# A two-part, four-layer transformer step: output products of the heads written feature-major, softmax scaling moved ahead of the transposes, lower weight halves written over the landed weights, splits three chunks ahead

## The chip, the cores and the metric

The kernel runs on one core of one Trainium2 chip. A core has TensorE (PE: matmul, with its weight loads shown apart as PEld), VectorE (DVE), ScalarE (ACT), GpSimd (POOL), SyncE (SP, here only the issuer of loads) and 16 DMA engines. Each engine works through its own list of instructions in order; they meet through semaphores. The metric is the device time of one execution in microseconds.

## The reference

Batch 1, 256 tokens, width 1024, float32. Part one has two layers, part two two more.

```
part one, per layer (first a layer norm of the input x):
  h = x @ w_in: differential heads (4 of 128), windowed heads with a bias (8 of 64),
      a gated 3-tap convolution, and 3 gates
  mix = sum over branches of sigmoid(gate_b) * (branch_b @ w_branch_b);  mix @ w_mix_out
  x = layer_norm(alpha*x + mix)
  cross-attention to mem (4 heads of 256: xa_q, xa_kv, xa_o);  x = layer_norm(alpha*x + .)
  ffn: silu(conv3(x@w_g)) * (x@w_u) @ w_out (inner width 2816);  x = layer_norm(alpha*x + .)
part two, per layer:
  x += 0.5 * swiglu(rms_norm(x));   x += 0.5 * swiglu(rms_norm(x))   (around the mixer)
  h = rms_norm(x) @ w_in_2: pooling, moba (4 heads of 64, causal here: one block of 256),
      dilated (4 heads of 64: 3 dilations merged in one softmax), 31-tap convolution module
  x += concat(pool, moba, dil, conv) @ w_out_2
out = rms_norm(x)
```

With 256 tokens the mask of a moba and of a dilated head is causal: queries 0 to 127 see keys 0 to 127 alone.

## The kernel before

**Weights as chunks.** All weights are cut into 336 chunks of 128 x 2048 float32 (1 MB), in order of use, and `mem` is one more chunk in each layer of part one. `plan()` (L97) lists the chunks and puts the heads' steps at chunk positions. A chunk is landed in `raw` by SyncE (L631), in one of three slots (`RING`, L32). ScalarE copies it to `whi` in the rounded matmul type fp32r (L728), VectorE subtracts to get the lower half `wlo` = `raw` - `whi` (L1317). TensorE then multiplies (L1022, `product`): for each block high x high, high x low and low x high, 48 matmuls of 128x128 by 256 columns for one chunk; all matmuls are recorded at the helper's line L989. Kind F gives features in rows, kind T tokens in rows, B and O are the branch and output products. An O chunk adds to the four banks of `accM`, one per pair of feature tiles.

**Who splits when.** While TensorE works on chunk `pos`, ScalarE and VectorE go through the same list: they take the result of chunk `pos-1` (`take`), do those steps of `pos` whose names are in `BEFORE_SPLIT`, split chunk `pos+2` (`split_at(pos + 2)`), and do the other steps. The second chunk after the last one of each group that ends in a norm (key `ends`) is split on GpSimd in place of VectorE (`by_pool`, L429 and L702), eleven in all. SyncE's load of chunk n waits until chunk n-3 is split.

**Norms.** At a chunk with `ends`, VectorE adds each of the four banks to x (L1357 in part one, L1360 in part two), ScalarE squares (L747), VectorE adds the squares (L1350). In part two the norm's scaling is put off to the results, and `xh`, `xl` (upper and lower half of x) are made at once (L741, L1335), so that the next chunk can start. In part one TensorE first sums x and the squares, spreads the factors, and x is scaled and shifted (L1395, L1401) before the next product.

**Heads.** A head has four steps, at positions one apart. *scores*: TensorE multiplies queries and keys, VectorE takes the maximum (for windowed, moba and dilated heads after adding a bias, L1639, L1642), ScalarE takes the exponential and sums each row in `ew` and `rsum` (L909). *turn*: TensorE transposes `ew`, four blocks of 128x128, into `turnP` (L1176); ScalarE copies it to `eT` (L915). *mix*: TensorE multiplies with `eT` as the weights and the values as the moving side, so that tokens stand in the rows; VectorE divides by the row sum (L1675, L1678) into `otok`. *back*: TensorE transposes `otok` into `outP` (L1203), for two heads of 64 features together; ScalarE and VectorE make the upper and lower half (L935; L1685, L1694) that the next product reads. A differential head scales `ew` by its row sums already after scores (L1651 to L1659), and has a norm of its own at mix.

TensorE's own steps of a position are spread over its product as hooks; those that the product needs (`needs`) come ahead of it. A bank is claimed by `Bank.claim`, which waits for its last reader. During O chunks the heads use the bank `outP`, since `accM` is taken.

**The second part's mixer** is the chunks `cg`, `ca`, `qm`, `km`, `qd`, `kd`, `up`, `vm`, `vd`, and then four of `wo`. VectorE also computes the 31-tap convolution there, in six groups of steps (`taps`, L1704; two operations per tap), one group at each of the positions `qm` to `vd`; on VectorE `taps` comes behind the split of its position. The convolution's own norm (`cstats`, `cspread`) uses `outP` at the first two `wo` chunks.

## Time and profile before

| | |
|---|---|
| three runs | 2282.15, 2287.42, 2293.49 us; median 2287.42 |
| profiled execution | 2269.32 us, its span 2267.5 us |
| TensorE | 2138.3 us busy, mean granted clock 0.974 |
| VectorE | 1436.8 us busy (63%) |
| ScalarE | 1009.3 us busy (45%) |
| GpSimd | 99.7 us busy (4%) |
| DMA | 366 MB, 161 GB/s over the span |

The rows used below name a line of the kernel, an engine, the operation, what it writes and what it reads, and how often. Matmuls overlap, so the duration of a single one is longer than its distance to the next. In a timeline "idle before" with an arrow says how long the engine had nothing to do and what ended that. The chain of waits is followed back from the last instruction; each of its pieces is a stretch in which one kind of work let the end wait.

### The profile page before, as it was taken

How to read it: one execution, taken by the hardware profiler on the slowest of the kernel's cores; microseconds unless marked ns; L12 is line 12 of the kernel's file. 1: busy time of each engine (PE TensorE's matmuls, PEld its weight loads, DVE VectorE, ACT ScalarE, POOL GpSimd, SP SyncE). 2: the span in 40 equal slices, each digit the busy share in tenths (PEclk: the TensorE clock that was granted, in tenths of full speed). 3: DMA queues.
4: the chain of work that ended last, by engine and by line, in shares of the span. 5: the costliest groups of instructions: out<-in, count | busy, mean ns of one | idle time of the engine just before them, and what ended most of it. 6: DMA issues, size and time to landing. Idle time of an engine off the chain costs nothing.

```text
span 2267.5 us, 39445 instructions
## 1 busy us (share of the span) xinstructions
PE 2138.3 (94%) x17460; PEld 2080.3 (92%) x17460; DVE 1436.8 (63%) x1690; ACT 1009.3 (45%) x1166; POOL 99.7 (4%) x69
## 2 busy tenths in 40 slices
PE   7999999899899999989997999879999999979998
PEld 6899999899899999989997999769999999868997
DVE  5665554666765656457776756866666666765665
ACT  4544454444445443544444434334444444234443
POOL 1000010100100000010001000001000000000000
PEclk9999999999999999999998999989999999989999
DMA  5444543355444455435552554323554555213542
GB/s 198 148 162 163 204 162 143 133 185 189 149 149 165 146 188 191 152 112 216 186 189 104 199 192 175 112 75 135 204 203 149 209 200 186 112 68 115 209 186 94
DMA packets 52858, 366.08 MB, mean 161 GB/s; under 512 B 5904, under 2 KB 5904, under 8 KB 9296
## 3 DMA queue, kind: packets, MB, share of 16 engines
q1 hardware_dynamic: 52272, 361.21, 43.3%
q8 instruction: 138, 2.26, 0.4%
q0 software_dynamic: 416, 2.35, 0.3%
q14 instruction: 32, 0.26, 0.0%
HBM read 362.49 MB, written 1.05 MB: 160 GB/s over the span
## 4 chain that ended last, share of the span: by engine, by line
PE 76%; DVE 10%; issue 9%; ACT 3%; POOL 1%; DMA 0%; POOLq 0%; ACTq 0%; DVEq 0%
PE accM L989 43%; PE scoreP L989 17%; PE outP L989 8%; PE turnP L989 7%; DVE wlo L1317 2%; DVE yc L1704 1%; ACT whi L728 1%; PE turnP L1176 1%; DVE xl L1335 1%; ACT ew L909 1%; DVE acc L1350 1%; PE outP L1203 0%; DVE cen L1395 0%; DVE cen L1401 0%; DVE mrs L1646 0%
## 5 line engine op out<-in xcount | busy, mean ns | idle before, releaser
L1317 DVE TENSOR_TENSOR wlo<-raw,whi 128x2048 fp32r<-128x2048 f32 x325 | 744.1, 2290 | 411.5 <-ACT whi L728 411.0
L728 ACT ACTIVATE whi<-raw 128x2048 fp32r<-128x2048 f32 x336 | 640.4, 1910 | 256.4 <-PE accM L989 169.9
L989 PE MATMUL accM<-xh,whi 128*128 128x256 f32 x1152 | 338.9, 294 | 16.8 <-DVE xl L1415 10.9
L989 PE MATMUL scoreP<-xh,whi 128*128 128x256 f32 x1152 | 325.9, 283 | 17.8 <-DVE xl L1415 9.0
L989 PE MATMUL accM<-xl,whi 128*128 128x256 f32 x1152 | 324.9, 282 | 0.0
L989 PE MATMUL accM<-xh,wlo 128*128 128x256 f32 x1152 | 324.9, 282 | 0.0
L989 PE MATMUL scoreP<-xl,whi 128*128 128x256 f32 x1152 | 323.7, 281 | 0.0
L989 PE MATMUL scoreP<-xh,wlo 128*128 128x256 f32 x1152 | 323.5, 281 | 0.0
L989 PE MATMUL accM<-fh,whi 128*128 128x256 f32 x1056 | 293.2, 278 | 0.7 <-DVE wlo L1317 0.7
L989 PE MATMUL accM<-fh,wlo 128*128 128x256 f32 x1056 | 293.1, 278 | 0.0
L989 PE MATMUL accM<-fl,whi 128*128 128x256 f32 x1056 | 293.1, 278 | 0.0
L989 PEld LDWEIGHTS accM<-xh,whi 128*128 128x128 f32 x1152 | 220.7, 192 | 27.6 <-issue 27.3
L989 PEld LDWEIGHTS scoreP<-xh,whi 128*128 128x128 f32 x1152 | 220.7, 192 | 19.4 <-issue 18.7
L989 PEld LDWEIGHTS accM<-xl,whi 128*128 128x128 f32 x1152 | 220.5, 191 | 2.7 <-issue 2.5
L989 PEld LDWEIGHTS accM<-xh,wlo 128*128 128x128 f32 x1152 | 221.9, 193 | 0.0
L989 PEld LDWEIGHTS scoreP<-xh,wlo 128*128 128x128 f32 x1152 | 221.7, 192 | 0.0
L989 PEld LDWEIGHTS scoreP<-xl,whi 128*128 128x128 f32 x1152 | 220.6, 192 | 0.2
L989 PEld LDWEIGHTS accM<-fh,wlo 128*128 128x128 f32 x1056 | 199.6, 189 | 0.0
L989 PEld LDWEIGHTS accM<-fh,whi 128*128 128x128 f32 x1056 | 198.2, 188 | 0.9 <-DVE wlo L1317 0.9
L989 PEld LDWEIGHTS accM<-fl,whi 128*128 128x128 f32 x1056 | 198.2, 188 | 0.0
L989 PE MATMUL turnP<-xh,whi 128*128 128x256 f32 x480 | 133.1, 277 | 0.0
L989 PE MATMUL turnP<-xl,whi 128*128 128x256 f32 x480 | 133.1, 277 | 0.0
(264 smaller groups left out, 4297.2 us busy)
## 6 DMA issues: line engine op xcount, KB each, us to landing
raw<-in_W SPq DMA_DIRECT2D x336, 1024.0 KB, 4.8
biasr<-in_bias SPq DMA_DIRECT2D x16, 256.0 KB, 2.7
raw<-in_memT SPq DMA_DIRECT2D x2, 1024.0 KB, 4.7
cc<-in_consts POOLq DMA_DIRECT2D x1, 1536.0 KB, 6.7
x<-in_xT SPq DMA_DIRECT2D x4, 256.0 KB, 4.4
out<-x SPq DMA_DIRECT2D x4, 256.0 KB, 2.5
c<-in_consts SPq DMA_DIRECT2D x1, 464.5 KB, 6.1
par<-in_par POOLq DMA_DIRECT2D x2, 203.5 KB, 3.7
```

What stands on the lines that cost most here:

```text
L728: nc.scalar.activation(whi[:, slot(c), :], raw[:, n % RING, :], ACT.Copy).then_inc(split_hi.sem, 1)
L909: ins = nc.scalar.activation(ew[:, e0 + i, :], src, ACT.Exp, bias=negmax[:, e0 + i:e0 + i + 1], scale=scale, accum_out=rsum[:, s0 + i:s0 + ...
L989: return nc.tensor.matmul(dst, a, b, start=start, stop=stop, skip_group_check=True)
L1176: ins = nc.tensor.transpose(turnP[:, k * S + t * P:k * S + (t + 1) * P], src[t][:, k * P:(k + 1) * P], ident)
L1317: v.tensor_tensor(wlo[:, slot(c), :], raw[:, n % RING, :], whi[:, slot(c), :].bitcast(F32), ALU.subtract).then_inc(split_lo.sem, 1)
L1335: ins = v.scalar_tensor_tensor(xl[:, k, :], x[:, k, :], gain(n, k), xh[:, k, :].bitcast(F32), ALU.mult, ALU.subtract)
L1350: v.tensor_tensor(accq, a, sq[:, b % 2, :], ALU.add).then_inc(summed.sem, 1)
L1704: ins = v.scalar_tensor_tensor(yc[:, m, :], src, w, yc[:, m, :], ALU.mult, ALU.add)
```

## The change

1. `raw` gets five slots and `whi` four. `wlo` also has five, and lies at the same addresses as `raw`: VectorE's subtract writes the lower half over the landed chunk. So the load of chunk n waits until the product n-5 is finished, not for a split.
2. Splits are made three chunks ahead (`LEAD`), two ahead at a chunk that ends in a norm. The second chunk after such a chunk then brings two splits. GpSimd splits no more; `by_pool` and `pool_lo` are gone.
3. Windowed, moba, dilated and cross-attention heads: VectorE multiplies `ew` by the inverse row sums at *turn* (new semaphore `evened`), and TensorE's transposes wait for it. At *mix* the values are the weights and `eT` the moving side, so that features stand in the rows. Two heads of 64 features share one bank, which turns with the banks of `accM` (`outP` in O chunks) and is kept until *back*. The scaling to `otok` and the transposes of *back* go; ScalarE and VectorE read the halves straight from the bank. Differential heads are unchanged.
4. Moba and dilated heads leave out the block of queries 0 to 127 against keys 128 to 255: scores, bias, exponential, transposes (three, not four) and the second matmul of the output product are that much smaller; the maximum is taken by two instructions in place of one.
5. In part two *back* moves from the third position after scores to the second, and what `wo` 1 and `wo` 2 need ahead of their product is now *mix*.

```diff
-RING = 3
+RAW_RING = 5
+HI_RING = 4
+LEAD = 3
...
+        raw = sb("raw", [P, RAW_RING, CH], where=landing)
+        landing.close()
+        wlo = sb("wlo", [P, RAW_RING, CH], F32R)
+        whi = sb("whi", [P, HI_RING, CH], F32R)
...
+                if name == "mix" and what["kind"] not in ("diff", "xa") and what["j"] % 2:
+                    mix_bank[what["n"]] = mix_bank[what["n"] - 1]
+                elif name == "mix" and c["kind"] in ("F", "T"):
...
+        def lead(pos):
+
+            return pos + LEAD - 1 if pos < len(chunks) and "ends" in chunks[pos] else pos + LEAD
...
-                if c["c"] >= RING:
-                    await_split(sp, c["c"] - RING)
+                r = raw_slot(c)
+                if c["c"] >= RAW_RING:
+                    old = chunks[c["c"] - RAW_RING]
+                    if old["kind"] == "M":
+                        await_split(sp, old["c"])
+                    else:
+                        await_chunk(sp, old)
...
-                if c["c"] + 2 in by_pool:
-                    n = c["c"] + 2
-                    pool.wait_ge(split_hi.sem, split_hi.at(n))
-                    nc.gpsimd.tensor_tensor(wlo[:, slot(chunks[n]), :], raw[:, n % RING, :],
...
-                    split_at(pos + 2)
+                    split_at(lead(pos))
...
-                        pe.wait_ge(expd.sem, expd.at(n))
+                        pe.wait_ge(evened.sem, evened.at(n))
...
+                            if kind in ("moba", "dil"):
+                                if k > t:
+                                    continue
+                                at = (k + t) * P
...
+                    elif kind == "xa":
+                        for d in range(2):
+                            for k in range(2):
+                                ins = mm(mix_bank[n][1][:, d * S:(d + 1) * S], v[:, k, v0 + d * P:v0 + (d + 1) * P],
+                                         e[:, k * S:(k + 1) * S], k == 0, k == 1)
+                    else:
+                        rows = slice(64 * (j % 2), 64 * (j % 2) + 64)
+                        late = P if kind != "win" else 0
+                        o = mix_bank[n][1]
+                        mm(o[rows, 0:S], v[:, 0, v0:v0 + w], e[:, 0:S], True, False)
+                        ins = mm(o[rows, late:S], v[:, 1, v0:v0 + w], e[:, S:2 * S - late], False, True)
...
+                mine = [s for s in steps.get(pos, []) if s[0] in PE_STEPS
+                        and (s[0] != "back" or s[1]["kind"] == "diff")]
...
+                elif name == "turn" and what["kind"] != "diff":
                     n, kind, j = what["n"], what["kind"], what["j"]
...
+                    dve.wait_ge(expd.sem, expd.at(n))
+                    s = mrs[:, 10 + 2 * (j % 2):12 + 2 * (j % 2)]
+                    i0 = sum_column(kind, j)
+                    v.reciprocal(s, rsum[:, i0:i0 + 2]).then_inc(inverted.sem, 1)
+                    dve.wait_ge(inverted.sem, inverted.at(n))
                     for t in range(2):
...
+                        e = ew[:, 2 * (j % 2) + t, keys(kind, t)]
+                        last = v.tensor_scalar(e, e, s[:, t:t + 1], None, ALU.mult)
+                    last.then_inc(evened.sem, 1)
```

## Rows read from the trace of the kernel before

**Rows 1.** The page, part 1: busy time and share of each engine.
```profile
...
PE 2138.3 (94%) x17460; PEld 2080.3 (92%) x17460; DVE 1436.8 (63%) x1690; ACT 1009.3 (45%) x1166; POOL 99.7 (4%) x69
...
```

**Rows 2.** The chain of waits, whole span: start us, us, work.
```profile
...
432.31 5.65 PE turnP L989 x48
...
1029.47 5.44 PE turnP L989 x48
...
```

**Rows 3.** Waits of TensorE, whole span: waited for, us in total, times, longest.
```profile
...
PE accM L989 <- DVE wlo L1317: 0.7, 1, 0.7
...
```

**Rows 4.** The page, part 6: KB of each load, us to landing.
```profile
...
raw<-in_W SPq DMA_DIRECT2D x336, 1024.0 KB, 4.8
...
```

**Rows 5.** Groups by line: out<-in, count, busy us, mean ns.
```profile
...
L1317 DVE TENSOR_TENSOR wlo<-raw,whi 128x2048 fp32r<-128x2048 f32 x325 | 744.1, 2290 | 411.5 <-ACT whi L728 411.0
...
L702 POOL TENSOR_TENSOR wlo<-raw,whi 128x2048 fp32r<-128x2048 f32 x11 | 50.6, 4602 | 1354.8 <-ACT whi L728 1354.8
...
```

**Rows 6.** Timeline at the norm ahead of a mixing stage: start, us.
```profile
...
1406.03 4.59 POOL L702 TENSOR_TENSOR wlo<-raw,whi 128x2048 fp32r<-128x2048 f32 x1 [176.49 <-ACT whi L728]
...
1407.41 3.89 DVE L1335 SCALAR_TENSOR_TENSOR xl<-x,par,xh 128x256 fp32r<-128x256 f32 x2
...
1411.82 0.87 DVE L1335 SCALAR_TENSOR_TENSOR xl<-x,par,xh 128x256 fp32r<-128x256 f32 x2
...
```

**Rows 7.** Timeline at a norm of part one.
```profile
...
1001.08 2.44 DVE L1350 TENSOR_TENSOR acc<-sq 128x512 f32<-128x512 f32 x1
...
1004.18 0.73 PEld L989 LDWEIGHTS turnP<-x,ones 128*128 128x128 f32 x4 [0.26 <-DVE x L1357]
...
```

**Rows 8.** Timeline around the transposes of cross-attention and window heads.
```profile
...
336.62 2.29 DVE L1317 TENSOR_TENSOR wlo<-raw,whi 128x2048 fp32r<-128x2048 f32 x1 [2.89 <-ACT whi L728]
...
354.83 0.69 DVE L1685 TENSOR_TENSOR ol<-outP,oh 128x512 fp32r<-128x512 f32 x1 [0.68 <-ACT oh L935]
...
354.20 0.59 ACT L935 ACTIVATE oh<-outP 128x512 fp32r<-128x512 f32 x1
...
122.28 0.48 DVE L1691 SCALAR_TENSOR_TENSOR yl<-outP,small,yh 128x256 fp32r<-128x256 f32 x1 [1.52 <-ACT yh L935]
...
122.29 0.60 PE L1176 MATMUL turnP<-c,ew 128*128 128x128 f32 x4
...
```

**Rows 9.** The chain of waits around heads.
```profile
...
338.46 0.44 PE turnP L1176 x4
...
344.56 1.73 PE scoreP L989 x8
...
124.94 1.06 PE scoreP L989 x4
...
134.17 4.62 PE accM L989 x38
...
```

**Rows 10.** Groups by line: VectorE's scaling operations.
```profile
...
L1655 DVE TENSOR_SCALAR ew<-ew,mrs 128x256 f32<-128x256 f32 x16 | 4.9, 350 | 0.3
...
L1675 DVE RECIPROCAL mrs<-rsum 128x2 f32<-128x2 f32 x40 | 6.6, 164 | 52.5 <-PE outP L989 31.8 <-PE accM L989 20.6
...
```

**Rows 11.** Timeline of the first mixing stage.
```profile
...
1474.00 4.54 DVE L1704 SCALAR_TENSOR_TENSOR yc<-hpad,par,yc 128x256 f32<-128x256 f32 x10
...
1474.81 0.99 PE L1176 MATMUL turnP<-c,ew 128*128 128x128 f32 x4 [3.98 <-ACT eT L915]
...
1520.61 0.69 PE L1203 MATMUL outP<-c,otok 128*128 128x128 f32 x2 [3.82 <-DVE yc L1719]
1525.00 1.30 PE L989 MATMUL outP<-v,eT 128*128 128x64 f32 x5 [3.69 <-DVE zl L1694]
...
1544.58 0.36 PE L989 MATMUL accM<-zh,whi 128*128 128x256 f32 x1 [1.02 <-DVE zl L1694]
...
```

**Rows 12.** Windows of the second mixing stage: busy us by engine, clock, DMA.
```profile
...
1979.00:1989.00 10.00, 5.22 (x36) 4.36 (x34) 6.93 (x10) 6.99 (x13) 0.00 (x0) 0.90 0.04 16
1989.00:1999.00 10.00, 10.00 (x35) 7.88 (x35) 6.34 (x13) 1.85 (x6) 0.00 (x0) 0.50 0.23 91
...
```

More of the change, by code:

```diff
@@ L70 @@
 NC0 = _at
-NC2 = 4 * 512 + 512 + 512
+TRI = P + S
+NC2 = 4 * 512 + 2 * TRI
 class Signal:
@@ L242, in plan @@
             at(base + 10, "cspread", l)
-            order = dict(rot=1, cstats=2, cspread=2, pool=2, back=3, mix=4, turn=5, scores=6, poolw=7, taps=8,
+            order = dict(rot=1, cstats=2, cspread=2, pool=2, mix=3, back=4, turn=5, scores=6, poolw=7, taps=8,
                          csquare=9)
@@ L262, in sem @@
             return ctx.enter_context(nc.semaphore(name))
-        raw = sb("raw", [P, RING, CH])
-        whi = sb("whi", [P, RING, CH], F32R)
-        wlo = sb("wlo", [P, RING, CH], F32R)
+        landing = ExitStack()
+        raw = sb("raw", [P, RAW_RING, CH], where=landing)
+        landing.close()
+        wlo = sb("wlo", [P, RAW_RING, CH], F32R)
+        whi = sb("whi", [P, HI_RING, CH], F32R)
         x = sb("x", [P, KT, S])
@@ L425, in kernel_program @@
         cs = [c["c"] for c in chunks]
-        landed = [sem(f"landed{i}") for i in range(RING)]
+        landed = [sem(f"landed{i}") for i in range(RAW_RING)]
         split_hi = sig("split_hi", cs)
-        by_pool = [c["c"] + 2 for c in chunks if "ends" in c and c["c"] + 2 < len(chunks)]
-        split_lo = sig("split_lo", [c for c in cs if c not in by_pool])
-        pool_lo = sig("pool_lo", by_pool)
+        split_lo = sig("split_lo", cs)
         def await_split(engine, c):
-            signal = pool_lo if c in by_pool else split_lo
-            engine.wait_ge(signal.sem, signal.at(c))
+            engine.wait_ge(split_lo.sem, split_lo.at(c))
         used = sig("used", [c["c"] for c in products if "ends" not in c])
@@ L506, in kernel_program @@
             for name, what, *_ in steps.get(c["c"], []):
-                if (name == "scores" and what["kind"] == "diff") or (name == "mix" and what["kind"] != "diff"):
+                if (name == "scores" and what["kind"] == "diff") or (name == "turn" and what["kind"] != "diff"):
                     inverse_order.append(what["n"])
@@ L513, in kernel_program @@
         weighed = sig("weighed", [n for n in stage["scores"] if hs[n]["kind"] == "diff"])
+        evened = sig("evened", [n for n in stage["turn"] if hs[n]["kind"] != "diff"])
         inverted = sig("inverted", inverse_order)
@@ L517, in kernel_program @@
         mixed = sig("mixed", stage["mix"])
-        oscaled = sig("oscaled", stage["mix"])
+        oscaled = sig("oscaled", [n for n in stage["mix"] if hs[n]["kind"] == "diff"])
         o2 = sig("o2", [n for n in stage["mix"] if hs[n]["kind"] == "diff"])
@@ L521, in kernel_program @@
         oroot = sig("oroot", [n for n in stage["mix"] if hs[n]["kind"] == "diff"])
-        backed = sig("backed", stage["back"])
+        backed = sig("backed", [n for n in stage["back"] if hs[n]["kind"] == "diff"])
         back_hi = sig("back_hi", stage["back"])
@@ L592, in head_place, with keys, laid @@
             return (zh, zl)[part][:, (2 if kind == "moba" else 4) + j // 2, :]
+        def keys(kind, t):
+            return slice(0, P) if t == 0 and kind in ("moba", "dil") else slice(0, S)
+        def laid(kind, t):
+            if kind in ("moba", "dil"):
+                return slice(0, P) if t == 0 else slice(P, TRI)
+            return slice(t * S, (t + 1) * S)
         def sum_column(kind, j):
@@ L860, in take @@
                 elif r == "su":
-                    split_at(pos + 2)
+                    split_at(lead(pos))
                     hidden(c)
@@ L1200, in step @@
                     pe.wait_ge(oscaled.sem, oscaled.at(n))
-                    for d in range(2 if kind == "xa" else 1):
-                        for t in range(2):
-                            ins = nc.tensor.transpose(outP[:, d * S + t * P:d * S + (t + 1) * P],
-                                                      otok[:, t, d * P:(d + 1) * P], ident)
+                    for t in range(2):
+                        ins = nc.tensor.transpose(outP[:, t * P:(t + 1) * P], otok[:, t, 0:P], ident)
                     ins.then_inc(backed.sem, 1)
@@ L1247, in needs @@
                 if c["role"] == "wo":
-                    return (name, what["kind"] if name == "back" else "") in {
-                        0: [("poolw", "")], 1: [("back", "moba")], 2: [("back", "dil")], 3: [("cspread", "")]}[c["j"]]
-                return c["role"] == "xo" and name == "back" and what["j"] == c["j"]
+                    return (name, what["kind"] if name == "mix" else "") in {
+                        0: [("poolw", "")], 1: [("mix", "moba")], 2: [("mix", "dil")], 3: [("cspread", "")]}[c["j"]]
+                return c["role"] == "xo" and name == "mix" and what["j"] == c["j"]
             hooks = {}
@@ L1316, in split @@
                     return
-                v.tensor_tensor(wlo[:, slot(c), :], raw[:, n % RING, :], whi[:, slot(c), :].bitcast(F32),
+                v.tensor_tensor(wlo[:, raw_slot(c), :], raw[:, raw_slot(c), :], whi[:, hi_slot(c), :].bitcast(F32),
                                 ALU.subtract).then_inc(split_lo.sem, 1)
@@ L1693, in step @@
                     else:
-                        v.tensor_tensor(lo, outP[:, 0:S], hi.bitcast(F32), ALU.subtract).then_inc(back_lo.sem, 1)
+                        v.tensor_tensor(lo, mix_bank[n][1][:, 0:S], hi.bitcast(F32), ALU.subtract)\
+                            .then_inc(back_lo.sem, 1)
                 elif name == "trig":
```

154 lines of the change are left out of this document (81 added, 73 removed).

## The prediction

> **What bounds the kernel now.** I read the page's busy shares first: TensorE works in 94% of the span [rows 1]. The chain of waits says how: in long stretches it is one product after another, 48 matmuls in 5.44 us in some of them and 5.65 us in others [rows 2]. At 5.44 us the 336 products need 1828 us of the 2267.5; 440 us are norms, heads, waits and the slower pace. The densest part of it is the mixing of the second part.
>
> Next the waits. TensorE waited for the lower half of a weight chunk once, 0.7 us in all [rows 3]. So deeper buffers and a third chunk of lead take away no wait that TensorE has. They can pay only through what moves with them.
>
> **Splits, rings and lead.** Five landing slots with the lower part written over them give the load of chunk n the start "product n-5 finished". Before it was "chunk n-3 split", which fell in about the same moment, but the split is now wanted a chunk earlier. A load lands 4.8 us after its issue [rows 4], a product lasts 5.44: ScalarE may wait up to 1 us for it, and TensorE wants the data three products later. I take 0, bounds 0 to +3 us, as the load just fits and the reserve of three products would have to be gone first.
>
> **The split leaves GpSimd.** Eleven lower halves were computed there, 4.60 us each [rows 5], at the moment when VectorE takes the norm's residual. They collide. In the second part GpSimd ran from 1406.03 to 1410.62 and VectorE's pair of `xl` operations took 3.89 us where its neighbours take 0.87 [rows 6]. The next product starts with this `xl`, so it is on the path. By the same row 3.0 us go at the norms that follow products 212, 258 and 291, and 2.0 at 225 and 304, where the collision is later: 13 us. In the first part an `acc` operation took 2.44 us in place of its normal 0.69 (what `x` and other operations of this size take), but TensorE was summing x meanwhile and waited 0.26 us for it [rows 7]. The squares come 1.8 us earlier, of which TensorE's own sums leave some 0.6: four norms make 2.4 us, and I give the two after `mo` nothing, since products lie beside them. Bounds for all six: 0 to 1.75 each.
>
> The Trainium skill (SBUF — State Buffer, "Who interferes with whom") states that a VectorE instruction with two SBUF inputs and a GpSimd instruction that reads SBUF exclude each other for the whole instruction. The trace agrees: the `xl` pair ends 0.7 us after GpSimd's subtract, while the residual with one input from PSUM beside it keeps 0.69 us. By the rule, the gain would be whole as soon as GpSimd has no such work, as I sum it.
>
> VectorE takes these eleven splits, 2.29 us each [rows 5]. They are done one chunk before the norm, and the place of the extra one is the catch-up: two splits in a row at the second chunk after the norm. In the feed-forward VectorE has room (63% busy over the span), so 0. In the mixing it has none; that is counted below.
>
> **Heads without the turn back.** Transposes cost TensorE 0.11 us each (four in 0.44) [rows 9]. Dropped: 4 per cross-attention head, 2 per pair of others. A cross-attention output product stays 8 matmuls of 256 columns. A window head's was 8 matmuls of 64 columns, 1.09 us (4.62 less 30 of a product at 0.1177); now it is 4 of 256 columns: between half of the 1.73 that eight take in cross-attention and the 1.06 of four score matmuls [rows 9]. So 0 to 0.2 us gained per head; I take 0.1.
>
> In exchange the transposes of every such head now wait for VectorE: reciprocal and two scalings (0.20, and twice 0.35 overlapping to 0.62, for 256 columns: 0.8 us; 0.76 where one is of 128) [rows 10]. What matters is what VectorE has queued before them.
>
> Cross-attention, first layer [rows 8]. Head 0: the transposes came at 338.46 [rows 9]; VectorE subtracts a weight chunk from 336.62 to 338.9 and is then ready with the head at 339.7: +1.3. Head 1: no transposes-back stand ahead any more, so its transposes move from the middle to the start of their product, about 353.5. But VectorE's program has the lower half of head 0 first, which waits for ScalarE's `oh`, and this for the copy of a product that ends only then: 354.83 + 0.69 + 0.8 = 356.3, a stall of 2.8, less 0.44 saved. Head 2 meets the same order with half a product in between: 1.5 late, less 0.44. The turns back of heads 2 and 3 save 0.9. Sum +3.8 a layer, **+7.6 us** for two; bounds 0 to +12.
>
> Window heads [rows 8]: head 0's transposes at 122.29 now wait behind `yl` (122.28 + 0.48), until 123.7: +1.3. Heads 3 and 5 meet `yl` in the same way, +0.4 each; the others have 1 to 2 us to spare. Less 0.9 for transposes and 0.8 for eight products: +0.4 a layer, **+0.8 us**; bounds -4 to +8.
>
> **The mixing stages** [rows 11]. From the norm ahead of the first (1407.41) to the start of its last product (1544.58) 137 us pass, in which 12 products need 65; the second is alike. At their start VectorE is the bound: each product brings a split (2.29), ten tap operations (4.54) and 1.4 to 2 us of rotation, over 8 us against a product's 5.44. The catch-up split comes there: +2.2 against the 3.0 that the norm gives back. Then the new wait bites. The transposes of moba 0 and 1 stood at about 1468.8 and at 1474.81; now they wait until VectorE has done a split (it may start when ScalarE is ready, about 1471), taps, a rotation and the scaling: 1479.0 and 1479.8. TensorE turns the second at 1480.8, +6.0. The scores behind come 4 to 5 us later, the transposes of moba 2 and 3 wait for the last taps (until 1495.2), and the product `vd` ends 4.7 late. From here it is regained. Triangular scores save 0.2 a head, the transposes 0.1, products some 0.4. Above all the turn back goes: before, TensorE waited 3.82 us for `outP` to be free for two transposes that it no longer has, then 3.69 us for `zl` behind the whole convolution norm, and 1.02 us at the last product. Now the convolution's spread goes about 3.2 late, at 1519.0. The first output product of the dilated heads follows the bank's release at about 1522.6 in place of 1525.0. `wo 1` ends at 1531.4 (before 1535.6), `wo 2` starts at 1538.3 (before 1544.6). So -6.3 in each stage, the norm's 3.0 included.
>
> The clock takes part of it back. In the second stage TensorE worked 5.22 of the 10 us from 1979, and in the 10 us after them it had a granted clock of 0.50, which is 1.2 GHz [rows 12]. Around the turns of moba 0 and 1 the first stage's idle time grows from 5 to 11 us, and I add 3 us there; the second paid that already. I take **-3.3 and -6.0**, bounds -12 to +5 each.
>
> **Sum**, against the profiled execution's own 2269.3 us: norms -2.4 and, outside the mixing, -3.0 -2.0 -2.0; cross-attention +7.6; windows +0.8; mixing -9.3. That is -10.3, or 2259. The other executions of before lie higher: the median is 2287.4, 18.1 above the profiled one. I lay the difference on the median: 2287.4 - 10.3, **2277 us**. The kernel's measurements can't tell less than about 0.5% (11.4 us) from no change, and this forecast lies just inside that.
>
> **Rivals.**
> (1) The waits hurt less, and GpSimd's collision more: VectorE gets through the mixing early enough, and only the gains are left (norms -15, mixing with -10 each, heads 0). The norm's 6 in the mixing is in both, so -29, of which 4 stay for windows and cross-attention: -25, 2262 us. For it: the pair of 3.89 us is ahead of TensorE's next product. Against it: the taps really stand ahead of the scaling in VectorE's program.
> (2) The scaling before the transposes costs more than the turn back gave. Its place is every non-differential head; its price per head is what VectorE has ahead, a split (2.29) or a group of taps (4.54). With 6 us more in each mixing stage, 6 in each cross-attention and 4 in each window stage, less the norms' 15, it is about +12 + 12 + 8 - 15 = +17 us: 2304. It decides once the late transposes of moba 2 and 3 carry on into the convolution's norm, that is if `cspread` comes more than 9 us late. For it: VectorE's queue is full there. Against it: the waits of 3.8 and 3.7 us stand right behind.
> (3) TensorE's pace. It ran the same feed-forward program at 5.65 us a product in the first layer and at 5.44 in the second (at 432.31 and 1029.47) [rows 2], and nothing in the chain says why. Six such stretches of 32 products are worth 6.7 us each. If two or three fall the other way, it is 2277 plus or minus 16.
> (4) The deeper lead does nothing and neither does the rest: 2287. That is near to my sum and can't be told from it by the time.
>
> **Chances.** Forecast, within 7 us of 2277: 0.40. Rival 1: 0.20. Rival 2: 0.15. Rival 3: 0.14, half each way. Rival 4: 0.11. Under 2276 (faster) lie rival 1, half of 3 and two fifths of the forecast's spread: 0.43. Over 2298.9 (slower): rival 2 and a little of 3: 0.17. The rest, 0.40, is within 0.5%. The range takes in rival 1 and ends just short of rival 2: 2257 to 2302; the likeliest case's own is 2270 to 2284.
>
> **What would show it.** Right: no VectorE operation of a norm longer than 1.5 us; TensorE waits for `ew` (the scaling) ahead of the head transposes, longest in the products `vm` and `vd` and at the second cross-attention head; no waits for `zl` and `otok` at `outP`; the stage from the last `sd` to `wo 2` 3 to 6 us shorter, cross-attention some 4 us longer. Wrong: TensorE waits for `wlo`, ScalarE idles before `whi` for a load by more than 1 us as a rule, the mixing grows longer than before, or the feed-forward products change their pace for good.

## The result, and the profile after

The change made the kernel slower. Median 2287.39 us in 20 runs (2271.17 to 2299.14), against 2270.74 us for the kernel before in 20 runs (2260.01 to 2293.49). The ratio is 1.0066, 95% interval 1.0044 to 1.0087, so +16.7 us between the medians. The forecast was 10.3 us faster. Its 2277 us lies within 11 us of the result only by luck: the difference was laid on a median of three runs, which 20 runs then put 16.7 us lower.

The profiled execution of after has a span of 2287.1 us, 19.6 more than before. The busy shares don't show it, as they stand where they stood [rows 1]:

```profile
PE 2143.3 (94%) x17252; PEld 2068.5 (90%) x17252; DVE 1435.2 (63%) x1717; ACT 1004.4 (44%) x1166; POOL 49.2 (2%) x58
```

The waits of TensorE do (waited for, us in total, times, longest; whole span):

```profile
PE turnP L1205 <- DVE ew L1721: 43.0, 14, 12.0
PE turnP L1012 <- DVE diag L1485: 18.7, 12, 3.0
PE accM L1012 <- DVE q L1585: 13.7, 4, 5.5
...
PE accM L1012 <- DVE wlo L1360: 4.1, 4, 1.0
```

The first row did not exist before: the transposes wait for the scaling, 43 us in 14 waits. Gone are the waits of before for `eT` (9.3 us), for `zl` at `outP` and at the last product (7.8 and 2.0) and for `yc` at the turn back (7.7), of which some came back elsewhere. Before, the last row was one wait of 0.7 us [rows 3]; in the kernel after it is four waits, at other products.

Where the 19.6 us are, from the starts of the 336 products in both traces (each stage from the start of one product to the start of a later one; products are numbered by chunk, as in the prediction):

| stage | before | after | difference | forecast |
|---|---|---|---|---|
| window heads, two layers | 83.2, 83.2 | 86.2, 86.1 | +5.9 | +0.8 |
| cross-attention, two layers | 107.8, 107.8 | 113.6, 113.5 | +11.5 | +7.6 |
| norms and seams of part one | | | +3.1 | -2.4 |
| norms after 225, 258, 304 | 15.1, 22.6, 15.1 | 13.1, 19.4, 13.1 | -7.2 | -7.0 |
| mixing, last `sd` to `wo 2` | 140.8, 148.0 | 140.6, 141.3 | -7.0 | -9.3 |
| catch-up in four feed-forwards of part two | | | +5.1 | 0 |
| pace of the feed-forwards | | | +7.3 | 0 |
| one gap gone (-1.0); start and end of the span (+0.2, +1.6) | | | +0.8 | 0 |

One trace of each kernel is not enough for the mixing row. The same mixing code took 140.8 and 148.0 us in the trace of before and 148.5 and 146.8 in that of E6 below, at granted clocks of 0.94, 0.87, 0.89 and 0.90 over the stage: 146.0 on average. In the four traces of the kernel after (E12 to E14 below are the same kernel) the eight stages took 140.6 to 141.7, 141.3 on average. By these the mixing became 4.8 us shorter in each stage, and the -0.2 of the first stage comes from an unusually short first stage of before.

**Norms.** In part two the forecast held. With GpSimd's split gone, VectorE's `xl` pairs of the norm ahead of the first mixing take 0.87 us each, none 3.89 [rows 6] (timeline of VectorE: start, us):

```profile
1424.41 0.68 DVE L1403 SCALAR_TENSOR_TENSOR x<-accM,x 128x512 f32<-128x512 f32 x1
1425.01 0.87 DVE L1378 SCALAR_TENSOR_TENSOR xl<-x,par,xh 128x256 fp32r<-128x256 f32 x2
1425.80 0.68 DVE L1403 SCALAR_TENSOR_TENSOR x<-accM,x 128x512 f32<-128x512 f32 x1
1426.40 0.87 DVE L1378 SCALAR_TENSOR_TENSOR xl<-x,par,xh 128x256 fp32r<-128x256 f32 x2
```

**The new wait in the mixing.** VectorE and then TensorE:

```profile
1486.64 2.29 DVE L1360 TENSOR_TENSOR wlo<-raw,whi 128x2048 fp32r<-128x2048 f32 x1 [2.85 <-ACT whi L748]
1488.85 4.54 DVE L1756 SCALAR_TENSOR_TENSOR yc<-hpad,par,yc 128x256 f32<-128x256 f32 x10
1493.43 0.69 DVE L1667 TENSOR_TENSOR k<-accM,k 128x512 f32<-128x512 f32 x1
1494.04 0.15 DVE L1717 RECIPROCAL mrs<-rsum 128x2 f32<-128x2 f32 x1
1494.23 0.55 DVE L1721 TENSOR_SCALAR ew<-ew,mrs 128x128 f32<-128x128 f32 x2
...
1494.92 0.88 PE L1205 MATMUL turnP<-c,ew 128*128 128x128 f32 x3 [11.99 <-DVE ew L1721]
```

This is the queue that the forecast named: split, taps and rotation stand ahead of 0.7 us of scaling, and TensorE stands still for 12 us. `vm` became 6.7 us longer (forecast +6.0) and `vd` behind it 3.4; `wo 0` then became 7.5 us shorter, as the turn back is gone.

**The catch-up.** VectorE two products after the norm behind product 225, in the kernel after, with TensorE's first `sd` matmul:

```profile
1582.90 4.49 DVE L1360 TENSOR_TENSOR wlo<-raw,whi 128x2048 fp32r<-128x2048 f32 x2 [2.58 <-ACT whi L748]
1587.31 0.69 DVE L1564 SCALAR_TENSOR_TENSOR fa<-fth,fa 128x512 f32<-128x512 f32 x1
1588.03 0.69 DVE L1567 TENSOR_TENSOR fu<-scoreP,rstdb 128x512 f32<-128x512 f32 x1
1588.75 0.69 DVE L1571 TENSOR_TENSOR fp<-fu,fa 128x512 f32<-128x512 f32 x1
1589.36 2.29 DVE L1360 TENSOR_TENSOR wlo<-raw,whi 128x2048 fp32r<-128x2048 f32 x1
1591.57 0.68 DVE L1616 SCALAR_TENSOR_TENSOR fl<-fp,fh 128x512 fp32r<-128x512 f32 x1
...
1592.35 0.36 PE L1012 MATMUL accM<-fh,whi 128*128 128x256 f32 x1 [1.02 <-DVE wlo L1360]
```

Two splits in a row (4.49 us) stand ahead of `fa`, `fu`, `fp` and `fl`. The row names `wlo` as what ended the wait, but `wlo` was done at 1591.65 and `fl` at 1592.25, 0.1 us before TensorE starts: the product waited for `fl`. The wait of 0.7 us of before [rows 3], on an `sd` product in the middle of a feed-forward, was another kind: there `wlo` did come last, 0.06 us ahead of TensorE. The deeper rings took this one away, with 1.0 us, where the prediction had said that they take away no wait.

**The window heads.** The output product before, then after, each with the product's next matmul; then VectorE and TensorE at head 0 in the kernel after:

```profile
127.45 1.00 PE L989 MATMUL accM<-vb,eT 128*128 128x64 f32 x8
128.26 0.36 PE L989 MATMUL accM<-xh,whi 128*128 128x256 f32 x1
```

```profile
122.54 0.48 DVE L1742 SCALAR_TENSOR_TENSOR yl<-outP,small,yh 128x256 fp32r<-128x256 f32 x1 [1.52 <-ACT yh L958]
122.94 0.15 DVE L1717 RECIPROCAL mrs<-rsum 128x2 f32<-128x2 f32 x1
123.13 0.62 DVE L1721 TENSOR_SCALAR ew<-ew,mrs 128x256 f32<-128x256 f32 x2
123.89 0.63 PE L1205 MATMUL turnP<-c,ew 128*128 128x128 f32 x4 [1.19 <-DVE ew L1721]
...
129.20 1.08 PE L1012 MATMUL accM<-eT,vb 128*64 128x256 f32 x4
130.21 0.38 PE L1012 MATMUL accM<-xh,whi 128*128 128x256 f32 x1
```

From start to the next matmul the eight matmuls of 64 columns take 0.81 us, the four of 256 take 1.01. With what the product around them loses in overlap a head is 0.28 us dearer (8.17 to 8.45 from product to product).

**The pace.** Two windows of 100 us of the kernel after, in the second and the third feed-forward of part two (TensorE busy, matmuls, clock, DMA):

```profile
1620.00:1720.00 100.00, 100.00 (x885) 1.00 0.54 193
1780.00:1880.00 100.00, 100.00 (x851) 1.00 0.51 181
```

Both are full and at full clock, yet 885 matmuls start in one and 851 in the other. Whole feed-forwards run at 5.44 or at 5.65 us a product. Before, the third one ran at 5.44. In the table above, pace is what the slower products cost, 0.21 us each. With it taken off the feed-forwards of both traces, after lies 12.3 us above before (spans of 2268.6 and 2256.3 us).

### The profile page after: what moved, and what is told of

Same layout as the page of the kernel before. It is cut to its first block, busy times and chain, and to the rows that moved or that the text cites. A ratio compares the mean times of both kernels' runs of the same rounds, so it can differ in the third digit from the quotient of the medians.

```text
span 2287.1 us, 39020 instructions
## 1 busy us (share of the span) xinstructions
PE 2143.3 (94%) x17252; PEld 2068.5 (90%) x17252; DVE 1435.2 (63%) x1717; ACT 1004.4 (44%) x1166; POOL 49.2 (2%) x58
## 4 chain that ended last, share of the span: by engine, by line
PE 72%; DVE 12%; issue 10%; ACT 4%; POOL 1%; DMA 0%; POOLq 0%; ACTq 0%; DVEq 0%
PE accM L1012 41%; PE scoreP L1012 16%; PE outP L1012 7%; PE turnP L1012 7%; DVE wlo L1360 4%; DVE yc L1756 2%; ACT whi L748 1%; PE turnP L1205 1%; ACT ew L930 1%; ACT xh L761 1%; DVE mrs L1696 0%; ACT sq L767 0%; DVE ew L1721 0%; DVE cen L1438 0%; DVE acc L1393 0%
## 5 line engine op out<-in xcount | busy, mean ns | idle before, releaser
L1360 DVE TENSOR_TENSOR wlo<-raw,whi 128x2048 fp32r<-128x2048 f32 x336 | 768.4, 2290 | 442.2 <-ACT whi L748 441.1
```

What stands on the lines that cost most here:

```text
L1360: v.tensor_tensor(wlo[:, raw_slot(c), :], raw[:, raw_slot(c), :], whi[:, hi_slot(c), :].bitcast(F32), ALU.subtract).then_inc(split_lo.sem, 1)
```

## The experiments

The stage times are worked out like those above. "Slow" counts the feed-forwards (of six) that ran at 5.65 us a product. The kernels of E1 to E4, of E5 to E8 and of E9 to E12 ran with the kernel before beside them, whose medians were 2270.98, 2278.11 and 2277.81 us. "Norm after 258" is the stage of that norm and the two products behind it.

| kernel | windows | cross-att. | mixing | norm after 258 | slow | profiled | ratio to before (95%) |
|---|---|---|---|---|---|---|---|
| before | 83.2 | 107.8 | 140.8, 148.0 | 22.6 | 2 | 2269.3 | 1 |
| after | 86.2 | 113.6 | 140.6, 141.3 | 19.4 | 3 | 2288.9 | 1.0066 (1.0044-1.0087) |
| E1 rings | 83.2 | 107.6 | 145.7, 148.3 | 19.4 | 3 | 2277.4 | 1.0006 (0.9977-1.0034) |
| E2 heads | 86.1 | 112.0 | 142.3, 142.3 | 22.5 | 4 | 2293.8 | 1.0061 (1.0033-1.0090) |
| E3 mixing only | 83.2 | 107.7 | 141.3, 141.3 | 19.5 | 2 | 2261.7 | 0.9960 (0.9933-0.9988) |
| E4 late catch-up | 86.0 | 113.6 | 139.7, 139.6 | 19.4 | 1 | 2265.5 | 0.9958 (0.9935-0.9982) |
| E5 both | 83.0 | 107.5 | 139.7, 140.1 | 19.6 | 2 | 2252.6 | 0.9868 (0.9829-0.9908) |
| E6 before + wait | 83.2 | 107.8 | 148.5, 146.8 | 22.5 | 2 | 2279.7 | 1.0020 (0.9990-1.0050) |
| E7 GpSimd scales, late | 85.5 | 107.7 | 127.9, 131.1 | 19.4 | 2 | 2240.1 | 0.9817 (0.9779-0.9854) |
| E8 no scaling | 84.3 | 106.1 | 131.1, 130.9 | 19.6 | 4 | 2255.7 | one run |
| E9 E7, token windows | 83.0 | 107.6 | 134.7, 131.4 | 19.4 | 2 | 2238.6 | 0.9806 (0.9764-0.9848) |
| E10 rings, late | 83.2 | 107.5 | 142.9, 143.7 | 19.4 | 1 | 2253.0 | 0.9887 (0.9852-0.9922) |
| E11 GpSimd scales | 85.8 | 106.1 | 130.6, 131.9 | 19.6 | 3 | 2250.8 | 0.9855 (0.9816-0.9893) |
| E12 after again | 86.2 | 113.5 | 141.2, 141.7 | 19.6 | 3 | 2288.1 | 1.0032 (1.0000-1.0065) |

**E1, the rings alone.** The kernel before with `RAW_RING = 5`, `HI_RING = 4`, `LEAD = 3` and all that goes with them, heads untouched.

> The kernel before with only the rings: five landing slots, lower half over them, four upper slots, lead of three chunks, no split on GpSimd; the heads as they were. Theory (the rings pay at the norms of the second part and cost at the catch-up): after against before the norms behind products 212, 258 and 291 are 3 to 4 us shorter and those behind 225 and 304 1 us, while four feed-forwards have a new gap of 1.3 us two products later and the first part's norms are 0 to 0.5 us longer. Sum about -5 us, ratio 0.998, and the windows and cross-attention as long as before. Rival (the rings are what made the kernel slower, through loads that are late): 5 to 15 us above before, ratio 1.003 to 1.007, with TensorE or ScalarE waiting for landed weights.

No difference that can be told (ratio 1.0006, interval 0.9977 to 1.0034; the medians are 6 us apart). The norms gained as expected. The mixing stages took 145.7 and 148.3 us, where the theory had left out that the catch-up's split stands there too, where VectorE is the bound: the product that meets it takes 12.16 us in place of 9.7 to 10.0 in both stages. The rest of the 4.9 us by which the first stage is longer is within the scatter of the mixing told above. No wait of TensorE for landed weights appears, so the rival falls.

**E2, the heads alone.** The other hunks of the change, on the old rings.

> The kernel before with only the heads changed: feature-major window, cross-attention, moba and dilated heads, scaling ahead of the transposes, triangular scores; rings of three and the split on GpSimd as before. Theory (heads cost the whole loss): windows +3.5 to +4 a layer, cross-attention +5.5 a layer, mixing between -2 and -5 a stage: +12 us, ratio 1.005. Rival (the parts hurt each other, the heads alone are harmless): ratio within 0.998 to 1.002.

Ratio 1.0061, as large as that of the whole change. Windows +2.9, cross-attention +4.2 and +3.9, mixing +1.5 and -5.7. With the slow pace taken off, its trace lies 11.7 us above before, and that of E1 1.2 us. Its own pace belongs to the result as well: four of six feed-forwards were slow, three of them in part two, though it has no catch-up.

**E3, only the mixing's heads feature-major.**

```
-                if name == "mix" and what["kind"] not in ("diff", "xa") and what["j"] % 2:
+                if name == "mix" and what["kind"] in FM and what["kind"] != "xa" and what["j"] % 2:
(FM = ("moba", "dil"); in the same way at the scaling, the bank's claim, the turn back and `needs`)
```

> The changed kernel with the window and cross-attention heads token-major again, their scaling behind the output product and turned back as before; only the moba and dilated heads are feature-major. Theory (new layout pays only in the mixing): 18.5 us below the changed kernel, so 2269, ratio to before 0.999. Rival (token-major heads suffer from the rings' VectorE order as well): less than 8 us below the changed kernel, ratio 1.003 or more.

It is 26 us below after by the medians (forecast 18.5), of which the stages give 17.7 (windows -5.9, cross-attention -11.8). The new layout loses in windows and cross-attention.

**E4, the catch-up later.**

```
             elif r == "su":
                 ...
                 split_at(lead(pos))
                 hidden_lo(c)
+                if j == 0:
+                    split_at(pos + LEAD)
(`lead` stays one lower up to there, in the mixing up to its eleventh product; the same on ScalarE)
```

> The changed kernel, but the extra split that brings the lead back to three after a norm of the second part comes later: in a feed-forward behind the first hidden group's lower half, in the mixing at its last but two product. Theory (the catch-up stands ahead of fl and of the first rotations): the gap of 1.2 us two products after each of the four norms goes (-4.8) and VectorE is 2.3 us less late in each mixing stage (-4.6): 9 us below the changed kernel, 2278, ratio to before 1.003. Rival (a shorter lead lets TensorE meet late splits elsewhere): no gain, ratio 1.006, with waits for wlo in the mixing.

The first `sd` product starts without a wait, as forecast. The mixing gains 0.9 and 1.7, less than the 2.3 forecast for each stage. VectorE now has the extra split behind `fl`:

```profile
1578.53 2.29 DVE L1367 TENSOR_TENSOR wlo<-raw,whi 128x2048 fp32r<-128x2048 f32 x1 [2.58 <-ACT whi L753]
...
1582.18 0.69 DVE L1578 TENSOR_TENSOR fp<-fu,fa 128x512 f32<-128x512 f32 x1
1582.80 2.28 DVE L1367 TENSOR_TENSOR wlo<-raw,whi 128x2048 fp32r<-128x2048 f32 x1
1585.00 0.68 DVE L1625 SCALAR_TENSOR_TENSOR fl<-fp,fh 128x512 fp32r<-128x512 f32 x1
1585.60 2.28 DVE L1367 TENSOR_TENSOR wlo<-raw,whi 128x2048 fp32r<-128x2048 f32 x1
```

But the median fell by 25.5 us, not by 9. In the trace 11.4 us remain with the slow pace taken off; the rest is pace: one slow feed-forward where after had three.

**E5, E3 and E4 together.**

> Both repairs together: only the moba and dilated heads feature-major, and the late catch-up. Without the two paces of TensorE the traces of the two single repairs lie 20 and 9 us below the changed kernel (products' starts, slow pace taken off). Theory (they add up): 29 us below the changed kernel by that measure, and with a pace like that of the late catch-up a median of 2241 to 2248, ratio to before 0.988 to 0.991. Rival (they overlap in the mixing, or the low median of the late catch-up was chance in the pace): 2252 or more, ratio 0.992 to 0.996.

The ratio is 0.9868, better than the theory's 0.988; the median of 2250.3 misses its 2241 to 2248, as the kernel before had a median of 2278 beside it and not 2271. With the slow pace taken off the trace is 30.5 us below after, and E3 and E4 together make 20.5 + 11.4. They add up.

**E6, the kernel before with a wait like the catch-up's.**

```
                     split_at(pos + 2)
+                    if j == 0:
+                        for _ in range(3):
+                            link(v.tensor_tensor(fp[:, :], fa[:, :], fa[:, :], ALU.mult))
                     dve.wait_ge(f_tanh.sem, f_tanh.at(c["c"]))
```

> The kernel before with three extra VectorE operations (2.2 us, their result is not used) in the first product group of each of the four feed-forwards of the second part, where the changed kernel has its extra split: the first sd product then waits about 1 us for fl. Theory (a wait of TensorE ahead of an undisturbed stretch draws its pace anew, 5.44 or 5.65 us a product, and what ran before it was mostly 5.44): 4 us for the waits and about 10 us more by slow stretches, ratio 1.004 to 1.008; in the trace about half of these stretches are slow from the first sd on, and no stretch changes pace without a gap. Rival (the pace has nothing to do with waits, the wait costs itself alone): ratio 1.001 to 1.0025.

Inconclusive: 1.0020 with an interval that holds both. Ahead of the first `sd` product TensorE is idle for 0.5 us in three of the four feed-forwards and for 1.0 in the fourth, and two of the four are slow. In before's own trace one was, and what its other executions had is not known.

**E7, the scalings on GpSimd, late catch-up.**

```
+                    if name == "turn" and what["kind"] != "diff":
...
+                        pool.wait_ge(expd.sem, expd.at(n))
...
+                        link(nc.gpsimd.tensor_tensor(inv, rsum[:, i0:i0 + 2], mone, ALU.pow))
+                        for t in range(2):
+                            e = ew[:, 2 * (j % 2) + t, keys(kind, t)]
+                            last = nc.gpsimd.tensor_scalar(e, e, inv[:, t:t + 1], None, ALU.mult)
+                        last.then_inc(evened.sem, 1)
```

> The changed kernel with the late catch-up, and all scalings ahead of the transposes on GpSimd (power of -1 and two multiplications) in place of VectorE. Theory (the new wait is the queue on VectorE, not the scaling): GpSimd has it 2 us after the exponentials; of the waits of the transposes (43 us in the changed kernel) more than half go, cross-attention is 3 us a layer and the mixing 4 us a stage shorter, windows the same. Rival (GpSimd and VectorE keep each other out): VectorE's splits and taps get longer by the scaling's time, transposes wait as long, mixing as long or longer.

Ratio 0.9817. The transposes wait 18.5 us in place of 43, the mixing stages are 12.7 and 10.2 us below after, cross-attention 5.9 a layer. By groups (count, busy, mean ns) GpSimd needs far longer than VectorE's 0.8 us a head (VectorE's scalings had a mean of 338 ns), and VectorE's splits and taps are what they were (2290 and 481 ns in after):

```profile
L732 POOL TENSOR_SCALAR ew<-ew,small 128x256 f32<-128x256 f32 (+1 forms) x80 | 104.9, 1322 | 4.0
L1379 DVE TENSOR_TENSOR wlo<-raw,whi 128x2048 fp32r<-128x2048 f32 x336 | 769.3, 2291 | 450.4 <-ACT whi L765 449.8
L1778 DVE SCALAR_TENSOR_TENSOR yc<-hpad,par,yc 128x256 f32<-128x256 f32 x120 | 53.1, 484 | 1.8
```

The first mixing stage in after, then in E7, as windows (busy us by engine, clock, DMA):

```profile
1420.10:1560.70 140.60, 112.22 (x774) 98.41 (x773) 95.64 (x181) 49.88 (x84) 1.38 (x2) 0.90 0.28 98
```

```profile
1404.80:1532.70 127.90, 108.44 (x774) 94.39 (x773) 91.07 (x157) 49.31 (x84) 26.05 (x26) 0.97 0.30 107
```

The granted clock of TensorE is 0.97 over the stage where it was 0.90, and its busy time 3.8 us less: that is part of the gain of 12.7.

**E8, no scaling at all.** The transposes wait for `expd` in place of `evened`; the division by the row sum is left out.

> The changed kernel without the division by the row sum in the window, cross-attention, moba and dilated heads (left out altogether); the transposes wait for the exponentials alone. Theory for the windows (the new output product of 256 columns is dearer than the old of 64, apart from any wait): of the 3.6 to 4.0 us a layer about 2 stay. Cross-attention: 5.5 us a layer dearer becomes 1 or more cheaper than before. Rival (all of the loss is the wait): the windows are back to or below their time before, 83.2 us. Mixing: 8 us or more a stage below the changed kernel.

It parts layout from wait, in one trace. Windows 84.3 and 84.5: of the 3.0 us a layer 1.1 to 1.3 stay, which is the wider output product less the turn back. The theory said about 2, the rival 0; it is between. Cross-attention 106.1, which is 1.7 below before: the four transposes a head that went. So its waits cost 7.5 a layer. Mixing 131: the waits cost 9.5 and 10.4.

**E9, the best of the stages together.** Windows and cross-attention token-major, mixing as E7.

> Window and cross-attention heads token-major, moba and dilated heads feature-major with their scaling on GpSimd, late catch-up. Theory (stages are independent): mixing stages as with the scaling on GpSimd (128 and 131 us from the last sd to wo 2), windows 83.1, cross-attention 107.6, so 5 us below the kernel with all scalings on GpSimd: 2230 to 2236, ratio to before 0.979. Rival (GpSimd's gain hangs on cross-attention and windows too): 2240 or more.

2238.45 us, ratio 0.9806: not measurably below E7 (0.9817), and above the 2230 to 2236 of the theory. The windows gave their 5 us. The first mixing stage was 6.8 us longer than in E7 at a granted clock of 0.91 over the stage in place of 0.97, the second about equal.

**E10, the rings with the late catch-up, heads as before.**

> The kernel before with the rings and the late catch-up, heads as before. Theory (the rings as such are worth the norms' 13 us, and lose them at the catch-up): 9 to 15 us below the rings alone, ratio to before 0.994 to 0.997; the first feed-forward products after a norm without a gap. Rival (the rings are worth nothing): ratio 0.999 or more.

Better than expected: 0.9887, or 25 us by the medians. The stages of its trace show some 11 us (norms, no gaps); the rest is put down to pace, as before had one slow feed-forward more in its trace. With the catch-up where VectorE has room the rings pay; where the change put it they were worth nothing that can be told (E1).

**E11, the scalings on GpSimd with the change's own catch-up.**

> The changed kernel with all scalings on GpSimd, and its own catch-up. Theory (scaling and catch-up are two separate losses): 33 us below the changed kernel without the pace, that is 2250, ratio to before 0.987 to 0.991; the gap of 1.2 us two products after the norms is there again. Rival (once VectorE has less to do the catch-up no longer costs): as low as with both, ratio 0.982.

0.9855. Its interval (0.9816 to 0.9893) holds the theory's and the rival's ratio. The trace decides for two separate losses: TensorE is idle again ahead of the first `sd` product of all four feed-forwards, for 0.6 to 1.0 us, and with the slow pace taken off the span is 5.2 us above that of E7.

**E12 to E16, the pace.** The changed kernel a second, third and fourth time, and E4's kernel a second and third time.

> The changed kernel as it is, beside the others on the same chip. Every theory: ratio to before 1.004 to 1.009, as measured first. What it adds is a second trace: which stretches of feed-forward run at 5.44 and which at 5.65 us a product. If a stretch has its pace from the instruction stream, the same ones are slow; if from the moment in which TensorE starts after a gap, others.

> The changed kernel, a third trace, for the pace of its four feed-forwards of the second part alone. If the catch-up's gap draws the pace anew with an even or worse chance: 2 or 3 of the 4 are slow (5.65 us a product) from the first sd product on. If the pace is blind to the gap: as many as without it, 0 to 2. The stages between agree with the first trace within 1 us.

> As the third trace: with the gap 2 or 3 of 4 stretches slow; blind to it, 0 to 2.

> The late catch-up, a second trace. If the gap is what draws the pace: 0 or 1 of 4 stretches slow (0 in its first trace). If the pace is blind to it: the same share as in the changed kernel, 2 or 3.

> As the second trace of the late catch-up: 0 or 1 of 4 slow, against 2 or 3 if the pace is blind to the gap.

The ratio of E12 was 1.0032 (1.0000 to 1.0065), under the forecast 1.004 to 1.009, into which its interval reaches. The stages agree from trace to trace (windows within 0.2 us, mixing within 1.1), the pace does not. In E12 the second feed-forward of part two, fast in the first trace of the same program, is slow (the chain of waits, two products):

```profile
1664.55 11.31 PE scoreP L1012 x96
```

Of the four feed-forwards of part two 2, 3, 3 and 3 were slow in the four traces of after, and 0, 1 and 1 in the three of E4. Over all traces: 24 of 36 slow where the catch-up's gap (or E6's) is there, 7 of 28 in those with the late catch-up. Before and E2 have neither: 1 and 3 of 4 are slow at their end. In all of them a stretch is slow or fast as a whole: from its last gap of TensorE on, the pace stays.

The same traces show where the draw falls. In the product just ahead of the gap, 8 of the 36 ran at the slow pace, much as without the gap; behind it 24 did. At the gap 20 of 28 went from 5.44 to 5.65 us a product, and 4 of 8 from 5.65 to 5.44. Of the 36 feed-forwards without the gap none changed pace at this place. The first feed-forward of part two in before and in E2 changed from fast to slow too, both at the one gap that they have in its middle, the 0.7 us of [rows 3] in before.

## Why the forecast was wrong

The forecast of -10.3 us and the +19.6 of the traces are 29.9 us apart, and no single term makes that up: 9.0 are the heads in windows and cross-attention, 5.1 the catch-up, 7.3 the pace, 5.5 the norms of part one, 2.3 the mixing. The steps that failed are these terms of the sum: the window's output product, priced as a gain; the clock behind the new waits of cross-attention, the catch-up and the pace, all three put at 0; and the gain at the norms of part one.

- **The heads in windows and cross-attention** cost +17.4 us where the sum had +8.4. The waits were named rightly in kind and place, and in the windows in size too (1.6 to 1.9 us a layer by E8, 2.1 in the sum). This is the largest term, and E2 shows that the heads alone make the kernel slower. In cross-attention the waits of the transposes are 5.3 us in the first layer, near to the 5.6 that I had (1.3 + 2.8 + 1.5). What the sum left out is what a wait does to the clock. Before, TensorE was busy throughout the stage and its clock 1.00 in every window. In after (windows: busy, clock):

```profile
341.00:351.00 10.00, 8.66 (x70) 1.00 0.36 111
351.00:361.00 10.00, 7.82 (x59) 1.00 0.36 122
361.00:371.00 10.00, 9.46 (x62) 0.83 0.24 91
```

  The last window is at 1.2 GHz for part of its time. Where this dip is missing (both layers in E2, one of the two in each of E13 to E16) the stage takes 111.7 to 112.0 us, with it 113.4 to 113.6. The difference lies in the one product behind the longest wait (7.08 us without it, 8.4 to 8.8 with it). Without the dip a layer is 4.0 us dearer, and the sum had 3.8. I had counted the half clock in the mixing [rows 12] and nowhere else.
- **The window's output product** was priced at 0 to 0.2 us gained per head, and with it a head costs 0.28 more. I had compared the wrong rows: 1.09 us for the old form, worked out as a remainder of the chain [rows 9], where the timeline has 0.81 from start to start. Four matmuls of 256 columns pass 1024 columns, eight of 64 pass 512. With the 0.9 us a layer for the turn back the sum had -1.7 here; E8 shows +1.1 to +1.3, 2.4 of the +5.9 us.
- **The catch-up** was put at nothing in the feed-forwards, because VectorE is 63% busy over the span. That is the average over stages that this kind of sum must not use: right there `fa`, `fp` and `fl` are a chain with 1.1 us of reserve, and 2.29 us were put into it. It cost 5.1 us by itself. E4 takes it away.
- **Pace** (rival 3) was held to be a coin that the change doesn't touch. The coin falls once more at each gap ahead of a long stretch, and the catch-up put such a gap ahead of four. By the counts above, against the late catch-up it is four stretches times (11/16 - 2/12) times 6.0 us, 12 to 13 us. Against the kernel before it is 7.3 us in the two traces, and how much of the 16.7 us between the medians it is, isn't shown: before has a gap of its own in one feed-forward, and in E2 three of four ran at 5.65 us without the catch-up's. That the pace is drawn at the gap is shown by the counts on both sides of it; what in the gap decides stays open, and E6 could not tell it.
- **Mixing**: -7.0 us in place of -9.3. `vm` late by 6.7 (forecast 6.0), then regained; the second stage -6.8 (forecast -6.0), the first -0.2 (forecast -3.3). By the averages of more traces it is -4.8 each, -9.5 in all, so the sum was right here. The way there was harder than forecast: in the first stage `vd` ended 8.8 us late (forecast 4.7), and the convolution's spread came 7.7 late (forecast 3.2), under the 9 that rival 2 asked for. More was then regained.
- **Norms of part two**: -7.2 us against -7.0, at each of the three places within 0.2. The Trainium skill's rule that this rested on (SBUF — State Buffer, "Who interferes with whom") was borne out there.
- **Norms of part one**: +3.1 in place of -2.4. The `acc` of 2.44 us did go, but it gave nothing: the last product ahead of a norm and the norm together took 19.84, 19.84, 20.43 and 19.67 us before at the four places of the forecast, and 19.92, 19.92, 20.22 and 20.27 after. TensorE waited 2.9 us for `diag` at the first of them in both. After `mo`, besides, VectorE's split now stands ahead of the residual and ends late, since ScalarE waited 3.6 us for the chunk to land. I had put the landing at 0, bounds 0 to +3. In the first layer the product ahead of the norm grew from 5.44 to 5.96 us. Why the four norms gave nothing stays open.

```profile
290.16 2.29 DVE L1360 TENSOR_TENSOR wlo<-raw,whi 128x2048 fp32r<-128x2048 f32 x1 [3.26 <-ACT whi L748]
292.37 2.07 DVE L1400 SCALAR_TENSOR_TENSOR x<-x,accM 128x512 f32<-128x512 f32 x3
```

- **Rival 2** named +17 us, and that is what was measured. Its terms say that this is luck in part: cross-attention +12 (measured +11.5) and windows +8 (+5.9) came about. Its +12 in the mixing did not (-7.0); in its place the catch-up and the pace brought 12.4.

## What to carry to other kernels

Ask of each operation that is added to an engine what stands behind it in that engine's program at that place, not how busy the engine is on average: 2.3 us in a chain with 1.1 us of reserve cost 1.2 us four times, and behind 0.7 us of scaling, which stood behind a split and a group of taps, TensorE stood still for 12 us (the waits of a mixing stage cost 9.5 to 10.4 us together, by E8). A slow but idle engine can be the better place for a short step that others wait for: GpSimd took four times as long for a scaling (1322 ns in place of 338), and the kernel, with the late catch-up, became 1.8% faster than before. Here a gap ahead of a long undisturbed stretch of TensorE mostly cost more than its length, so judge such a change by several traces.

## What the runs showed of the hardware

- The same stream of matmuls of 256 columns runs at 113.3 or at 117.7 ns from start to start (48 in 5.44 or 5.65 us), at a granted clock of 1.00 in both. The Trainium skill (TensorE: Matmul & The Clock Gate, "Back-to-back issue gap") gives N / 2.4 + 2.5 ns as the isolated gap between matmuls at the full clock, and says that a stream of weight loads and matmuls departs from it. At 256 columns the formula makes 109 ns, an estimate from that page; both measured paces are longer. A feed-forward of part two keeps one of the two from its last gap to its end. Where TensorE was idle for 0.5 to 1.0 us ahead of its first `sd` product, 8 of 36 feed-forwards were slow just before that gap and 24 of 36 behind it. Without the gap 7 of 28 were slow with the late catch-up, and 4 of 8 in before and E2, two of these four from a gap further on.
- GpSimd's two scalings and VectorE's split can get into each other's way. In E11 the pair took 1.83 us, and the split that began in it took 2.55 us in place of 2.29:

```profile
338.58 1.83 POOL L727 TENSOR_SCALAR ew<-ew,small 128x256 f32<-128x256 f32 x2
339.55 2.55 DVE L1372 TENSOR_TENSOR wlo<-raw,whi 128x2048 fp32r<-128x2048 f32 x1 [2.89 <-ACT whi L760]
```

  In E7, at the same place of the program, the split took its 2.29 us, and the pair 3.97:

```profile
338.93 3.97 POOL L732 TENSOR_SCALAR ew<-ew,small 128x256 f32<-128x256 f32 x2
339.90 2.29 DVE L1379 TENSOR_TENSOR wlo<-raw,whi 128x2048 fp32r<-128x2048 f32 x1 [2.90 <-ACT whi L765]
```

  This made cross-attention 107.7 us in E7 and 106.1 in E11: the product with these transposes took 7.70 and 6.20 us, the others were alike. In both traces the second scaling is recorded as starting 0.06 us ahead of the split, so the recorded starts don't tell which of the two gives way. The rule of the Trainium skill named above is that one of the two has the shared ports for the whole instruction. E7 fits it. In E11 the split overlapped the second scaling for 0.86 us and became only 0.26 us longer, which is less than the rule would give. The 80 scalings on GpSimd cost VectorE nothing that its mean durations show, and keeping them off GpSimd for fear of such meetings would have been a loss.
